# Hand-overs of a three-stage expert layer: query scores to the up products, up products to the down products

## The reference, cut to what matters

```
q = (h @ w_q).reshape(t, 8, 2, 128)
sc = einsum('thpc,hpnc->thpn', q, subkeys)
s1, i1 = top_k(sc[:, :, 0], 16);  s2, i2 = top_k(sc[:, :, 1], 16)
top_s, top_p = top_k(s1[..., :, None] + s2[..., None, :], 16)
experts = e1 * 128 + e2;  gates = softmax(top_s)
pre = einsum('td,tkd->tk', x, u_tab[experts])
act = gelu(pre) * gates
y = einsum('tk,tkd->td', act, v_tab[experts])
x = x + y;  out = rms_norm(x)
```

## Time and profile before

| | us |
|---|---|
| median of 3 runs | 2885.43 (2876.87 to 2885.61) |
| the profiled execution, its own time | 2886.46 |
| its span from first to last instruction | 2884.7 |
| TensorE busy | 2718.0 (94% of the span) |
| VectorE busy | 2304.1 (80%) |
| ScalarE busy | 1262.0 (44%) |
| GpSimd busy | 1436.9 (50%) |
| mean granted TensorE clock | 0.975 |

### The profile page before, as it was taken

One profiled execution on the slowest core, in us unless ns is written; L12 is line 12 of the kernel. 1 busy time (PEld: TensorE's weight loads), 2 busy tenths in 40 slices (PEclk: granted clock), 3 DMA queues, 4 the chain that ended last, 5 costly groups with the idle time before them and its releaser, 6 DMA issues. The chain is left out here.

```text
span 2884.7 us, 39998 instructions
## 1 busy us (share of the span) xinstructions
PE 2718.0 (94%) x14923; PEld 2379.0 (82%) x14923; DVE 2304.1 (80%) x4084; ACT 1262.0 (44%) x2538; POOL 1436.9 (50%) x934
## 2 busy tenths in 40 slices
PE   7999799979999998999999999986999999999998
PEld 6777566449999998999999999985788887788777
DVE  3284796329979899888889887877899989998987
ACT  4244342123322222988898889852222222222222
POOL 1021320004338674666667666663565656666653
PEclk9999798989999999999999999998999999999999
DMA  4110100223228884999999999999999999999995
GB/s 121 37 40 20 59 1 22 88 66 104 65 89 294 286 280 160 371 382 391 374 398 382 387 367 394 393 382 364 355 381 387 379 364 350 365 377 370 369 362 199
DMA packets 332098, 762.66 MB, mean 264 GB/s; under 512 B 23216, under 2 KB 158384, under 8 KB 329344
## 3 DMA queue, kind: packets, MB, share of 16 engines
q0 software_dynamic: 111104, 403.02, 37.4%
q1 hardware_dynamic: 138080, 314.48, 29.6%
q10 hardware_dynamic: 82720, 42.60, 5.3%
HBM read 667.73 MB, written 92.27 MB: 263 GB/s over the span
## 5 line engine op out<-in xcount | busy, mean ns | idle before, releaser
L1946 POOL DMA_INDIRECT v_rows<-in_peer_v,row_numbers x336 | 537.6, 1600 | 369.9 <-DVE y_rest L2023 229.4
L1585 PE MATMUL expert_pre<-h2T,uT_hi 128*128 128x320 f32 x4096 | 672.6, 312 | 5.8 <-ACT uT_hi L1619 5.8
L1701 POOL DMA_INDIRECT u_rows<-in_peer_u,row_numbers x384 | 538.6, 1403 | 253.0 <-DVE row_weights L1722 177.0
L1585 PEld LDWEIGHTS expert_pre<-h2T,uT_hi 128*128 128x128 f32 x4096 | 613.1, 189 | 6.0 <-ACT uT_hi L1619 6.0
L1722 DVE CUSTOM_DVE_ANT_0 u_rows<-u_rows,h_rows_kept 128x1024 f32<-128x1024 f32 x384 | 482.4, 1275 | 131.7 <-DMA u_rows<-in_peer_u,row_numbers 129.6
L2077 PE MATMUL expert_out<-v_hi,w_hi 128*128 128x512 f32 x1280 | 504.1, 394 | 50.1 <-DVE w_lo L2001 32.3
L2077 PE MATMUL expert_out<-v_lo,w_hi 128*128 128x512 f32 x1280 | 502.0, 392 | 0.0
L2077 PE MATMUL expert_out<-v_hi,w_lo 128*128 128x512 f32 x1280 | 501.4, 392 | 0.0
L1585 PE MATMUL expert_pre<-h2T,uT_lo 128*128 128x320 f32 x2048 | 345.5, 310 | 19.9 <-DVE uT_lo L1789 16.9
L2023 DVE SCALAR_TENSOR_TENSOR y_rest<-v_rows,row_weights,y_rest 128x1024 f32<-128x1024 f32 x256 | 326.4, 1278 | 38.2 <-DMA v_rows<-in_peer_v,row_numbers 36.0
L1970 ACT ACTIVATE w_hi<-pick_memory 128x640 fp32r<-128x640 f32 x128 | 94.8, 741 | 566.5 <-DVE pick_memory L1994 543.5
(11 more groups left out here) (322 smaller groups left out, 4120.3 us busy)
## 6 DMA issues: line engine op xcount, KB each, us to landing
u_chunk<-in_peer_u_turned SPq DMA_DIRECT2D x128, 512.0 KB
pick_memory<-in_peer_v SPq DMA_DIRECT2D x128, 512.0 KB
gates_dram<-pick_memory SPq DMA_DIRECT2D x20, 2048.0 KB
pick_memory<-acts_dram SPq DMA_DIRECT2D x128, 320.0 KB
pick_memory<-gates_dram ACTq DMA_DIRECT2D x32, 1280.0 KB
acts_dram<-expert_acts SPq DMA_DIRECT2D x126, 320.0 KB
wq_tile<-in_peer_wq SPq DMA_DIRECT2D x32, 512.0 KB, 3.9
w_in_columns<-in_w_in SPq DMA_DIRECT2D x20, 512.0 KB, 4.0
```

What stands on the lines that cost most here:

```text
L1585: last = nc.tensor.matmul(pre[:, (2 * c + half) % 4, 0:WIDTH], part[:, c % 2, k], m.h2T[:, t, k, HALVES[half]], start=n == 0, stop=n == le ...
L1701: pool.indirect_dma_start(rows[:, k % RING], None, table, bass.IndirectOffsetOnAxis(ap=m.row_of[:, f, slot:slot + 1], axis=0)).then_inc(fe ...
L1946: pool.indirect_dma_start(rows[:, k % ROW_RING], None, d.peer_v, bass.IndirectOffsetOnAxis(ap=m.row_of[:, f, slot:slot + 1], axis=0)).then ...
```

## The change: what it does

- **Score to up.** The query weights' tiles (`wq`, `wq_hi`, `wq_lo`) live on into `experts_up` and serve as two of the three places of a `u` chunk and as its high and low parts. SP loads chunks 0 and 1 at the end of `score`, and ACT and POOL make the high and the low part of chunk 0 there.
- **Key stage.** `decode_heads` works in bf16 for the dense tiles; the transpose of a tile's keys stands four quarters later (`TURN_AFTER` 22 for 18), and so does the first spread group (`SPREAD_FROM` 168 for 164).
- **End of up.** The last row is due two quarters earlier; ACT stores the acts of the last four chunks instead of two and the last part of the gate table; the loads of the gates are SP's instead of ACT's, and the first one is cut in two: 19 parts as soon as they are stored, the last part later. `pick_memory` is cut up anew so that the gates of even groups lie in the first spread buffer.
- **Down.** In the first group there are no gathered rows, neither fetched nor added; DVE multiplies a chunk's acts before it makes `v_lo`; the loads of `y` (the residual) come after the loads of chunk 4 and of chunk 6 instead of at once, and DVE waits for them later. The 336 rows are spread over groups 1 to 30 instead of 0 to 30.

The core of the diff:

```diff
@@ score, sync / gpsimd / scalar
+                for c in range(2):
+                    sp.wait_ge(lo_done, 2 * HP - 1 + c)
+                    sp.dma_start(w[:, c], d.peer_u_turned[c]).then_inc(m.u_in[c], 16)
...
+                pool.wait_ge(m.uhi_done, 1)
+                pool.tensor_tensor(wlo[:, 0], w[:, 0], whi[:, 0].bitcast(F32), ALU.subtract).then_inc(m.ulo_pool, 1)
...
+                act.wait_ge(m.u_in[0], 16)
+                act.wait_ge(query_done, items_through(2 * HP - 2))
+                A(whi[:, 0], w[:, 0], ACT.Copy).then_inc(m.uhi_done, 1)
                 scores_out(2 * HP - 1)
@@ experts_up
-    KEYS_FROM, SPREAD_FROM, SPREAD_TO = 136, 164, QUARTERS - 12
-    EARLY_DOTS, ROWS_TO = 72, QUARTERS - 4
-    LEAD, U_RING, ACT_STORES = SLOTS - 1, 3, 2
-    KEY_STEPS, TURN_AFTER = 7, 18
+    KEYS_FROM, SPREAD_FROM, SPREAD_TO = 136, 168, QUARTERS - 12
+    EARLY_DOTS, ROWS_TO = 72, QUARTERS - 6
+    LEAD, ACT_STORES = SLOTS - 1, 4
+    KEY_STEPS, TURN_AFTER = 7, 22
...
-        decode_wide = [m.pick_memory[:, i * WIDE:(i + 1) * WIDE].rearrange("p (h n) -> p h n", h=PH) for i in range(3)]
+        decode_wide = [m.pick_memory[:, i * WIDE:i * WIDE + WIDE // 2].bitcast(BF16).rearrange("p (h n) -> p h n", h=PH)
+                       for i in range(3)]
...
                 sp.wait_ge(spread_stored[0], 16 * (ALL // PART // 2))
-                sp.wait_ge(spread_read, ALL)
-                for x in range(DOWN_LOADS - 1):
+                for x in range(2):
                     load_v(sp, d, m, x)
-                for x in range(DOWN_LOADS):
                     load_acts(sp, d, m, x)
+                load(NK - 1)
+                load_gates(sp, d, m, 0, slice(0, ALL // PART - 1))
                 sp.wait_ge(spread_stored[1], 16 * (ALL // PART // 2))
-                load_v(sp, d, m, DOWN_LOADS - 1)
+                load_gates(sp, d, m, 0, slice(ALL // PART - 1, ALL // PART))
+                load_acts(sp, d, m, 2)
+                load_v(sp, d, m, 2)
+                load_acts(sp, d, m, 3)
+                load_gates(sp, d, m, 1)
...
-                    if q == QUARTERS - 6:
-                        for b in range(2):
-                            act.wait_ge(spread_stored[b], 16 * (ALL // PART // 2))
-                        load_gates(act, d, m, 0)
-                    if q == QUARTERS - 1:
-                        load_gates(act, d, m, 1)
                     for g in groups_at(q):
                         spread_out(g)
+                        if g == ALL - 1:
+                            act.wait_ge(spread_read, ALL)
+                            act.dma_start(d.gates[g // PART].rearrange("p e t -> p (e t)"),
+                                          spread[:, g // PART % 2].rearrange("p e t -> p (e t)")
+                                          ).then_inc(spread_stored[g // PART % 2], 16)
@@ experts_down
                     load_v(sp, d, m, x)
-                    load_acts(sp, d, m, x)
-                    if x == DOWN_LOADS:
-                        sp.dma_start(m.y_rest[:, 0:F - 1], d.x2[P:F * P].rearrange("(t p) n -> p t n", p=P)
-                                     ).then_inc(y_in, 16)
+                    if x + 1 < NK:
+                        load_acts(sp, d, m, x + 1)
+                    if x == C:
+                        for b in range(2):
+                            sp.wait_ge(m.act_stored[b], 16 * NK // 2)
                         sp.dma_start(m.y_rest[:, F - 1:], d.x2[F * P:].rearrange("(t p) n -> p t n", p=P)
                                      ).then_inc(y_in, 16)
+                    if x == C + 2:
+                        sp.dma_start(m.y_rest[:, 0:F - 1], d.x2[P:F * P].rearrange("(t p) n -> p t n", p=P)
+                                     ).then_inc(y_of_rows_in, 16)
+                    if x % C == C - 2 and 2 <= x // C + 1 < NG:
+                        load_gates(sp, d, m, x // C + 1)
...
-                asked = lambda x: min(ROW_RING + max(x - C, 0) * AXPYS // (NK - 2 * C), AXPYS)
-                for k in range(asked(0)):
-                    fetch(k)
+                asked = lambda x: min(ROW_RING + max(x - 2 * C, 0) * AXPYS // (NK - 3 * C), AXPYS) if x > C + 1 else 0
...
-                    if c == 0 and 1 <= n < NG - 1:
-                        load_gates(act, d, m, n + 1)
...
-                added = lambda s: min(s * AXPYS // ((NG - 1) * BANKS), AXPYS)
+                added = lambda s: min(max(s - BANKS, 0) * AXPYS // ((NG - 2) * BANKS), AXPYS)
```

More of the change, by code:

```diff
@@ L1536, in load @@
                         wait_low(sp, c - U_RING)
-                    sp.dma_start(u[:, c % U_RING], d.peer_u_turned[c]).then_inc(u_in[c % U_RING], 16)
-                for c in range(U_RING):
+                    sp.dma_start(u[c % U_RING], d.peer_u_turned[c]).then_inc(u_in[c % U_RING], 16)
+                for c in range(2, U_RING):
                     load(c)
@@ L1702, in fetch @@
                         ap=m.row_of[:, f, slot:slot + 1], axis=0)).then_inc(fetched[k % RING], 16)
-                low(0)
                 for q in range(QUARTERS):
@@ L1923, in _ @@
             def _(sp):
-                for x in range(DOWN_LOADS, NK):
+                for x in range(V_RING, NK):
                     if x == NK - 2 * C:
@@ L2027, in _ @@
                 for x in range(C):
+                    multiply(x)
                     low_of_v(x)
-                    multiply(x)
                     low(x)
-                dve.wait_ge(y_in, 32)
                 def vary(e):
```

56 lines of the change are left out of this document (31 added, 25 removed).

## The result

| | us |
|---|---|
| before, median of 4 runs | 2885.52 (2876.87 to 2887.81) |
| after, median of 4 runs | 2841.15 (2830.98 to 2847.36) |
| ratio | 0.9829, interval 0.98 to 0.9859 |
| the profiled execution after, its own time | 2830.98 (before 2886.46) |
| its span | 2829.2 (before 2884.7) |

A forecast was written before the change was run, and what follows sets the result against it. TensorE, DMA engines and VectorE were about equally tight inside the stages, leaving four TensorE holes, 43.8 us. Sum: 2886.5 - 4.5 - 9.9 + 1 - 3.5 - 9 + 5 = 2865.6, stated as 2865; range 2843 to 2882.

The forecast's parts named there:

- Score to up: End of `score`: TensorE's hole shrinks from 5.79 to 2.4 us, most slow restart spared; 4.5 us gained, bounds 2.3 and 4.8.
- Key stage: TensorE's 8.55 us wait for VectorE's `route` closes through four later quarters and bf16 decode; 9.9 us gained, bounds 8.4 and 9.9.
- End of up: SP asks for `v` and acts ahead of the last chunk of `u`; 1 us lost, bounds 0 and 5.
- First matmul of down: Between up and down: ACT no longer stuck, `v_lo` off the path; 3.5 us gained, bounds 0 and 6.
- First group: First group of down: without rows the wait for turned banks shrinks; 9 us gained, bounds 3 and 18.
- Groups 1 to 31: Rest of down: 11.2 rows a group against gates leaving ACT's queue; 5 us lost, bounds 16 lost and 8 gained.
- Fewer queues serve the rows better: Rival for down: first-group gain at 18, no loss in the groups, giving 2852 us; chance 0.22.
- no second hole: Part of the 2852 us rival: TensorE has no wait in down's first group, the first-group term at 18; chance 0.22.
- The DMA engines set the pace: Rival for down: engines bound it to the end, its hand-over gives nothing back, giving 2873 us; chance 0.18.
- A gate load on SP's queue holds up `v`: Rival for down: `v` comes late group after group; at 2 us late the time is 2921; chance 0.06.
- did what it says in the early part: Denies a rival: TensorE held as long as before in the early part, nothing gained in down, 2880 to 2886; chance 0.06.
- The time of 2905: Down's groups at 358 GB/s of HBM: 29.6 us a group, 39 us more over 30 groups, ending near 2905 us.

The follow-up runs named there:

- experiment 5: After, with group 2's gate load and the second load of `y` behind chunk 7's `v` instead of ahead of it: 2830.66 us, ratio 0.98.
- b_gates_on_sp: The kernel before with one part alone, the gate loads of groups 2 to 31 on SP's queue instead of ACT's: 2852.47 us, ratio 0.987.
- experiment 1: The run a_gates_on_act: after, with the gate loads of groups 2 to 31 back on ACT's queue: 2879.83 us, ratio 0.996.
- experiment 3: Before, with gates on SP and acts on ACT's queue in larger packets: 2874.64 us; or gate loads on ACT's queue reading 2560-byte pieces of `v`: 2861.19 us.
- experiment 6: After, with group 2's gate load behind chunk 7's `v`, both `y` loads behind chunk 4, rows from mid first group: 2826.68 us, ratio 0.9789.
- a_gates_on_act: After with one part undone, the gate loads of groups 2 to 31 on ACT's queue again: 2879.83 us, ratio 0.996.

## Why the prediction was wrong, point by point

**Score to up: right, the size 1.0 too large.** The term was 4.5 us. The hole shrank by 3.5, to 2.28 (forecast 2.4). The 1.4 us of slow restart were not spared: 5.12 us for the first 24 matmuls behind a hole of 2.28 us, 4.94 behind one of 5.79, at a mean granted clock of 0.67 and 0.70. The shorter hole did not keep the clock up.

**Key stage: right.** 9.9 us forecast, about 10 found; no hole, as said. That the sizes agree to the decimal is luck, given the spread of up. The later quarters alone left 4.02 us and not 1.5, so the bf16 decode was needed for more than the prediction said.

**End of up: about right.** I charged 1 us, with bounds of 0 and 5. Up took 1078.0 us in after and 1077.8 to 1083.6 in its five relatives, mean of the six 1079.5, where before with the key stage alone has 1075.4: some 4 us. The four kernels with before's up differ by 8.6 among themselves, so that this is no firm number. Which of the other edits costs them was not tried.

**First matmul of down: right mechanism, too small.** The term was 3.5, the measured 6.0, at the bound. I had left VectorE's last gathered row at its old moment, 2 us behind TensorE. It came along with everything ahead of it and was due two quarters earlier; it was added by 1922.80 and held nobody. The matmul came 5.66 us behind the last of up, where I had said 7 to 9.

**First group: right mechanism.** I forecast a hole ended by chunk 7's `v`, under 10 us; it was 10.54, and the gain 6.1 for 9. Experiment 5 shows that the loads ahead of that `v` were its cause. But the worth of the hole was misread: removed, it gives nothing by itself while 11.2 rows stand in each group behind it.

**Groups 1 to 31: this is the step that failed.** The term was a loss of 5, with a gain of 8 as its better bound; the measurement is a gain of 24.9 in the profiled pair (27.4 us a group over 2000 to 2800, where I had said 28.2 to 28.7), and 32 of down's 930.9 for the queue alone. The prediction put it so: "It had 369", and weighed what a group would take at 369 against 383. Both halves were wrong in kind. I treated 369 GB/s as a ceiling of the stage, and it was the result of the waits: with rows late, VectorE late and TensorE late, everyone asks later. Nor was 383 a limit for the better case: 10.59 MB in a group of 27.5 us is 385 GB/s, and after moved that, 385 over 2100 to 2700 us. The prediction's own working at 383 gave a gain of 18, and I still set the bound at 8 and gave no reason. And the rows that could have told it were at hand: one packet of q10 for one of q1, a gate load of 38.8 us, rows late 24 times. I used them for the gates' own lateness, and charged the rows' with nothing. What the runs showed in its place: with the gates in SP's queue, waits for rows fall from 45.6 to 11.4 us (`b_gates_on_sp`), and the groups run at TensorE's pace while the engines move 383 GB/s. The time of a gather was the tight thing, not the bandwidth. With this term at -24.9 and the others as they were the sum is 2835.7.

**The rivals.** "Fewer queues serve the rows better" names the cause; it had a chance of 0.22 and the price of a bound, 14 us in all, less than half of what the queue is worth. Its "no second hole" did not happen and was not needed. "The DMA engines set the pace" looks like what happens with the gates left on ACT's queue (experiment 1), where the gains of the hand-over were given back; but the engines moved only 367 GB/s then, so it was late rows again and not the engines' rate that held the stage. "A gate load on SP's queue holds up `v`" did happen, once, in the first group where `v` had no lead; in the groups a load lands in 17.1 us, inside the 20.6 of lead, as estimated (19.5). ACT did wait for `v` there, 38.0 us in 19 times between 2000 and 2800 where in before it never did, but it had the time: TensorE lost 3.7 us to `w_lo` in the stretch for 20.6 in before. The change did what it says in the early part.

**Bandwidth and turns.** The prediction set the 358 GB/s per core of the Trainium skill ("DMA: Bandwidth & Descriptors", Specifications) against the trace. The stage moved 379 GB/s over 800 us. The time of 2905 was also added up wrongly: 39 us in place of the loss of 5, not on top of it, give 2900, 59 us off. The Trainium skill's page "HBM Reference", Specifications (TRN2), says that a core that streams alone gets well above that share, about 425; the runs here agree with the direction, at 379 to 383. On turns the rule of the Trainium skill ("DMA: Bandwidth & Descriptors", Queues, rings and completion order) is that an engine goes round the queues that have work; the 1178 packets of q10 beside 1173 of q1 agree. The number of queues alone does not price it: in experiment 3 a third queue with large packets cost less than one with small ones. "Rules for kernel authors" of the same page of the Trainium skill say that spreading transfers over more engines brings no bandwidth and saves issue time alone; the runs agree that it brings none, and the spread cost 37 us here.

## What to carry to other kernels

Where DMA engines are full, ask of each queue who can wait and who can't, not only how many bytes there are: a stream with a fixed number of transfers in flight can't wait, and here a third queue, with many small packets, took 1.3% of the kernel by making it late. A rate read from a stage in which engines wait is no ceiling; work out what the stage would ask for without its waits (here 385 GB/s), and take that as the better bound. And a hole that is closed ahead of a stage with no slack can come back inside it: experiment 5 closed 10 us and gained nothing that could be measured, while experiment 6, which also thinned the rows from 11.2 to 11.0 a group, kept 7.4 us of down.

## What the runs showed of the hardware

- An issue can stand still behind a large load in the same queue: SP 13.82 us behind a gate load of 2560 pieces, ACT 10.30 us in before. Whatever stands behind in that engine's program waits too.
- The same 1280 KB load landed in 17.1 us (median) in SP's own queue and in 26.6 as the third queue, though no other load stood ahead of it there (after and `a_gates_on_act`, 2100 to 2700 us).
- TensorE's first 24 matmuls behind the hole at the end of `score` took 4.94 to 5.62 us in all thirteen traces, whether the hole was 2.3 or 5.8 us long, and the next 24 took 3.52.
- Some of VectorE's operations take 2 to 4 us where their like take 0.2 to 1.3 (the 3.83 us for 1.23 above), some at the same places in every run and some at others; the cause was not looked for. Score began between 626.4 and 633.4 us in kernels with the same work ahead of it. Terms of 2 to 4 us can't be read from one pair of traces.
